# A loop of six turns for TensorE's value matmuls of the second token tile, and six diagonal buffers in place of four

## The reference

```python
ug = u_tab[ec]
vg = v_tab[ec]
act = jax.nn.gelu(jnp.einsum('thkd,td->thk', ug, xc).astype(jnp.float32), approximate=False)
w = (gc * act).astype(vg.dtype)
return jnp.einsum('thk,thkd->td', w, vg)
```

## Time and profile before

| what | value |
|---|---|
| time, median of 3 runs | 1499.05 us (1497.91 to 1499.57) |
| the profiled execution's own time | 1500.34 us |
| span of the profile of that execution | 1498.5 us |
| PE busy, share of the span | 1372.7 us, 92% |
| DVE busy | 788.3 us, 53% |
| gathers (DMA queue q0), share of 16 engines' span | 44.0% |

### The profile page before, as it was taken

One profiled execution on the slowest core, in us unless ns is written; L12 is line 12 of the kernel. 1 busy time (PEld: TensorE's weight loads), 2 busy tenths in 40 slices (PEclk: granted clock), 3 DMA queues, 4 the chain that ended last, 5 costly groups with the idle time before them and its releaser, 6 DMA issues.

```text
span 1498.5 us, 16481 instructions
## 1 busy us (share of the span) xinstructions
PE 1372.7 (92%) x6098; PEld 709.4 (47%) x6098; DVE 788.3 (53%) x1912; ACT 292.7 (20%) x714; POOL 349.1 (23%) x321
## 2 busy tenths in 40 slices
PE   6999999999999999999999999997997777778787
PEld 4887665443443443433566665543543233333332
DVE  2257665232332332323525788757676766767555
ACT  1435312000000000001324433221212121212112
POOL 0005303000000000000000346543544443444450
PEclk9999999999999999999999999999999998998999
DMA  9743789999999999999343699999999999999997
GB/s 382 301 160 128 282 331 354 400 427 426 426 423 425 424 426 427 426 426 426 141 168 113 247 421 420 420 421 421 421 421 420 422 421 422 421 421 422 421 421 290
DMA packets 65442, 551.32 MB, mean 368 GB/s; under 512 B 9265, under 2 KB 9537, under 8 KB 11857
## 3 DMA queue, kind: packets, MB, share of 16 engines
q1 hardware_dynamic: 26944, 278.06, 45.2%
q0 software_dynamic: 38416, 272.17, 44.0%
HBM read 549.16 MB, written 1.05 MB: 367 GB/s over the span
## 4 chain that ended last, share of the span: by engine, by line
PE 66%; DMA 28%; issue 2%; DVE 2%; ACT 1%; POOL 1%; SPq 0%; POOLq 0%; DVEq 0%; ACTq 0%
DMA ring<-peer_uv_d,work 18%; PE ps L2117 14%; PE ps L2015 12%; PE ps L2170 7%; PE ps L1354 6%; DMA work<-peer_uv_d,work 4%; PE ps L1843 4%; PE ps L1348 4%; PE ps L1804 4%; PE ps L2127 4%; DMA ring<-w_ada_d 2%; PE ps L1670 2%; DMA work<-expert_w_d 2%; DMA consts_sb<-peer_uv_d,work 1%; PE ps L1584 1%
## 5 line engine op out<-in xcount | busy, mean ns | idle before, releaser
L2015 PE MATMUL ps<-ring,work 128*128 128x512 f32 x604 | 288.1, 628 | 64.1 <-ACT work L1285 63.0
L3398 DVE CUSTOM_DVE_ANT_0 ring<-ring,work 128x1024 f32<-128x1024 f32 x152 | 186.7, 1229 | 121.4 <-DMA ring<-peer_uv_d,work 120.6
L2015 PEld LDWEIGHTS ps<-ring,work 128*128 128x128 f32 x604 | 116.8, 200 | 223.4 <-issue 136.3
L2350 POOL DMA_INDIRECT ring<-peer_uv_d,work x149 | 169.5, 1138 | 201.7 <-PE ps L2015 163.2
L2117 PE MATMUL ps<-ring,work 128*64 128x512 f32 x704 | 181.6, 592 | 0.5 <-DVE work L2914 0.5
L2015 PE MATMUL ps<-work 128*128 128x512 f32 x272 | 126.1, 610 | 21.6 <-ACT work L1285 21.6
L1285 ACT ACTIVATE work<-consts_sb,work 128x128 f32<-128x128 f32 x256 | 85.1, 392 | 280.2 <-DVE work L3407 278.9
L2117 PEld LDWEIGHTS ps<-ring,work 128*64 128x64 f32 x704 | 60.0, 137 | 99.7 <-issue 99.7
L3398 DVE CUSTOM_DVE_ANT_0 work<-work 128x1024 f32<-128x1024 f32 x68 | 83.3, 1225 | 45.3 <-DMA work<-peer_uv_d,work 44.7
L2322 POOL DMA_DIRECT2D mod<-subkeys_d x1 | 0.5, 546 | 454.9 <-DVEq L3006 454.9
L1354 PE MATMUL ps<-ring,hT 128*128 128x512 f32 (+1 forms) x256 | 105.7, 567 | 0.0
(11 more groups left out here) (500 smaller groups left out, 1809.8 us busy)
## 6 DMA issues: line engine op xcount, KB each, us to landing
ring<-expert_w_d SPq DMA_DIRECT2D x66, 2048.0 KB, 20.9
work<-expert_w_d SPq DMA_DIRECT2D x33, 1024.0 KB, 21.5
ring<-w_ada_d SPq DMA_DIRECT2D x12, 2048.0 KB, 9.9
ring<-w_in_d SPq DMA_DIRECT2D x11, 2048.0 KB, 20.5
consts_sb<-expert_w_d SPq DMA_DIRECT2D x11, 1024.0 KB, 20.0
ring<-w_out_d SPq DMA_DIRECT2D x4, 2048.0 KB, 8.1
mod<-expert_w_d SPq DMA_DIRECT2D x8, 1024.0 KB, 18.7
hT<-expert_w_d SPq DMA_DIRECT2D x8, 1024.0 KB, 21.1
```

Source lines behind the costliest of these rows:

```text
L2015: last = pe.matmul(ps[V_BANK[t] + n][:, :], diag[:, i % 4, :], v_row(i)[:, n * 512:(n + 1) * 512], start=(i % (16 * PH) == 0), stop=(i == ...
L2350: pool.indirect_dma_start(out=uv_rows(i), out_offset=None, in_=io["peer_uv"], in_offset=bass.IndirectOffsetOnAxis(ap=idx[:, s, k:k + 1], a ...
L3398: dve.tensor_tensor_reduce(out=u_row(i), in0=u_row(i), in1=h_tok[:, i // (16 * PH), :], scale=1.0, scalar=0.0, op0=ALU.mult, op1=ALU.add, ...
```

## The change

TensorE's picks 144 to 251 are no longer written out. `TURNED` is 256 - 3 - 1 - 108 = 144, and a loop of six turns (`TURNS`) goes over the 18 places. The 18 picks of the body wait for `diag_ready` at a value that is computed in a register from the turn. The argument `head_slot` asks that the loop's first instruction be loaded at the start of a block of instructions; a branch leads over the padding ahead of it. Picks 252 to 255 follow written out, as before. Since 18 is not a multiple of four, the body would need other buffers in each turn; there are now six diagonal buffers (`DIAGS`), and ScalarE waits for the pick six before. The `else` branch gets the same loop, and is not run.

```diff
+TURNS = 6
+TURNED = 16 * TT * PH - APART - 1 - UV_PLACES * TURNS
...
+DIAGS = 6
...
-        diag = W(6144, 4, P)
+        diags = [W(6144, 4, P)[:, i, :] for i in range(4)] + [W(12976, 2, P)[:, i, :] for i in range(DIAGS - 4)]
...
-                        if i + k - k0 > 3:
-                            act.wait_ge(v_free, i + k - k0 - 3)
-                        act.activation(diag[:, k % 4, :], ident, ACT.Copy,
+                        if i + k - k0 >= DIAGS:
+                            act.wait_ge(v_free, i + k - k0 - DIAGS + 1)
+                        act.activation(diags[(i + k - k0) % DIAGS], ident, ACT.Copy,
...
-                            last = pe.matmul(ps[V_BANK[t] + n][:, :], diag[:, i % 4, :], v_row(i)[:, n * 512:(n + 1) * 512],
+                            last = pe.matmul(ps[V_BANK[t] + n][:, :], diags[i % DIAGS], v_row(i)[:, n * 512:(n + 1) * 512],
...
-                values(at, 16 * N_STEP)
+                values(at, TURNED)
+                with nc.Fori(0, TURNS, engines=bass.OrderedEngineSet([pe.engine]), head_slot={pe.engine: 0}) as turn:
+                    for i in range(TURNED, TURNED + UV_PLACES):
+                        pe.wait_ge(diag_ready, turn * UV_PLACES + (i + 1))
+                        for n in range(2):
+                            last = pe.matmul(ps[V_BANK[1] + n][:, :], diags[i % DIAGS],
+                                             v_row(i)[:, n * 512:(n + 1) * 512], start=False, stop=False,
+                                             skip_group_check=True)
+                        last.then_inc(v_free, 1)
+                values(TURNED + UV_PLACES * TURNS, 16 * N_STEP)
```

More of the change, by code:

```diff
@@ L369 @@
 UV_PLAN = uv_plan(16 * TT * PH)
+TURNS = 6
+TURNED = 16 * TT * PH - APART - 1 - UV_PLACES * TURNS
+assert TURNED > 8 * TT * PH and all(UV_PLAN[i][0] == UV_PLAN[i + UV_PLACES][0]
+                                    for i in range(TURNED, TURNED + UV_PLACES * (TURNS - 1)))
+DIAGS = 6
+assert UV_PLACES % DIAGS == 0
 UV_TURN = [sum(UV_PLAN[m][0] == UV_PLAN[i][0] for m in range(i + 1)) for i in range(len(UV_PLAN))]
```

## The result

The changed kernel takes 1503.88 us (median of 22 runs, 1498.31 to 1505.65), the kernel before 1498.96 us (22 runs, 1497.91 to 1503.27). The ratio is 1.0023, with an interval of 1.0016 to 1.003: slower by about 3.4 us, where 1499.1 us was forecast. Of the 22 of the kernel before, one is above 1502. The profiled execution of the changed kernel took 1503.73 us, and its span is 1501.9 us, 3.4 us more than that of the profile before (whose execution, 1500.34 us, was itself 1.4 us above its median).

A forecast was written before the change was run, and what follows sets the result against it. DMA engines, full with gathers, were taken as the bound. Span 1498.5 us plus 0 (fetches, branches, registers) and 0.1 (end) made 1498.6; 1.84 around it, less 1.29 to the median, gave 1499.1 us, range 1497.2 to 1501.4.

The forecast's parts named there:

- the span of 1498.5 us: Whole program: the earlier profile's span, taken as the starting value to which the gather stage's terms were added.
- Fetches of code, gain 0: Gather stage: three TensorE code fetches fall on a DMA engine with time left; gain 0, at the other end 3.5 us.
- Rival C: Gather stage: the code fetches did cost, 1.15 us each, and three are gone; 1495.6 us, chance 0.05.
- Branches, 0 in the first five turns: TensorE's loop in the gather stage: 0.05 us a branch, at most 3.57 us, hidden by TensorE's rest; cost 0.
- The upper bound of 3.57 us: TensorE's loop branches: most one might take, from TensorE's own jump over the other branch at 1493.7 us.
- Register instructions: TensorE's loop: 18 register additions are 0.67 us a turn, at most 5.4 us, under the 9.5 us of rest; cost 0.
- The sixth turn, 0.1 us: End of the gather stage, where picks run without a pause: delays add up to 0 to 0.2 us, taken as 0.1.
- Rival B: End of the gather stage: a branch or register waits are dear, up to 2.1 us; 1500.5 to 1501.2 us, chance 0.08.
- The last jump: TensorE's jump at its end: still there, with 1.0 us to spare before SyncE's drain; no change.
- Six diagonals, 0: Gather stage: diagonals wait for VectorE's weights, so more buffers don't bring them earlier; 0.
- Rival A: Gather stage: as forecast, all hidden; 1499.1 us, 1497.9 to 1500.3 with scatter, chance 0.80.
- Rival D: Gather stage: TensorE's back edge waits for its code behind the gathers, up to 74 us slower, 1573 us; chance 0.03.

The follow-up runs named there:

- experiment 3: Changed kernel with the loop replaced by written-out picks in both branches, six diagonal buffers kept: 1498.9 us, ratio 1.0002 to the kernel before.
- experiment 1: Two added waits make GpSimd's first sums wait for VectorE: changed kernel 1499.11 us, ratio 0.9996; kernel before 1499.45 us, 1.0006.
- experiment 2: Kernel before with one added wait: VectorE starts two masks only when ScalarE has scaled the tile GpSimd then sums; 1505.19 us, ratio 1.0041.
- experiment 4: Changed kernel with the loop in one branch, the other written out: only where it runs 1503.9 us, ratio 1.0018; only where never run 1504.23 us, 1.0019.
- experiment 7: Never-run matmuls added: changed kernel (288) 1498.92 us, ratio 0.9993; loop only in the branch not run (160) 1499.2 us, 0.9994; kernel before (288) 1499.12 us, 0.9994.
- experiment 9: Changed kernel with both two waits added on GpSimd and 288 matmuls that never run: 1499.63 us, ratio 0.9996 to the kernel before.

## Why the prediction was wrong

The step that failed is its first sentence: "The change touches one stage, so I read the busy time by stretches first". All terms of the sum and all four rivals lay in the stage of the gathers, and the span of 1498.5 us went into the sum as it was: everything outside the stage was put at 0 without a reason. The runs showed in its place a loss in the head of the program, where the kernel before stood about 0.2 us (0.51 less the 0.30 us from mask to mask) from a meeting that costs 4.3 us. By TensorE's first matmul of the experts it had grown to 5.5 us, and 3.4 us were left at the end of the profile.

- *Fetches of code, gain 0:* right. The q8 packets fell from 51 to 49; from 1231 to 1492 us one is left, at the start of the loop, where the earlier trace rows has three. The dots stayed 2.48 us apart (1303.80 to 1306.28 after), and the step of the earlier trace rows stands as before, 3.39 us (1341.09 to 1344.48). Rival C is out: TensorE's code is fetched less and nothing was gained.
- *Branches, 0 in the first five turns:* right in the sum, too small in the size. The prediction took 0.05 us, and under 0.1 us as the sign of being right; a back edge took 0.21 to 0.23. The upper bound of 3.57 us did not hold the branch in, which took 5.41 us. Both are hidden. TensorE's run of 16 matmuls ahead of the loop began at 1221.35 and the loop's first at 1231.28, 9.93 us apart; the same two stand 9.92 us apart before (1217.90 and 1227.82). The run took 8.60 us, at a granted clock of 0.83, where it took 7.13 us at 1.00 before, and even so ScalarE's diagonal is what TensorE waits for in both.
- *Register instructions:* 32 ns each; no gap of the dots or of TensorE grew by them.
- *The sixth turn, 0.1 us:* 191.61 against 191.60 us from a dot to the last additions, so 0. The branch passed takes 76 ns, and TensorE rests 0.88 us before pick 253, as in the earlier trace rows (0.90). Rival B is out.
- *The last jump:* 3.64 us in place of 3.57, still hidden.
- *Six diagonals, 0:* right, by experiment 3.
- *Rival A* described its stage rightly and missed the time. *Rival D* gave the sign that was found, by luck, for a reason that was not: from issue to landing a gather takes 25.6 to 32.8 us, as in the earlier trace rows.

What stands in place of the failed step, and how far each link goes. That the loss is the meeting of two engines is shown from both sides: taken away with the loop in place (experiment 1), and made without it (experiment 2). That it comes with the length of TensorE's code, or with something that goes with it, whether run or not, is shown by experiments 4 and 7, with one gap: neither the filled kernels nor that with the waits ran beside the changed kernel as it is, and only their ratios to the kernel before link them. That the link between them is the landing of the weights fits all 15 profiles, since GpSimd came at most 0.25 us after the start of the first mask wherever they met, and at least 0.41 us after it wherever they did not; but each kernel has one profile, and no run moved the landing alone in a controlled way. How the length of code moves a landing by some tenths of a microsecond stays open. Open too is the rest of the scatter: executions above 1502 us are found of the kernel before as well, 17 of 136 over all comparisons, and no profile shows one of them. Some are left where GpSimd is made to wait, too (1 of 11 and 1 of 12, experiments 1 and 9), so this meeting isn't their only cause.

## What to carry to other kernels

A change that makes the program shorter can move the time in a part of the kernel that it doesn't touch: lay the two traces side by side from the start and look for the first row that differs, before looking at the code that was changed. Where GpSimd's sums run beside VectorE instructions with SBUF inputs, read the distance of their starts; if it is tenths of a microsecond, order them by a semaphore (here it cost nothing that the runs show, 1.0006), since otherwise each small edit may decide anew whether they meet. And when the runs of a kernel fall into two groups, compare how many fall into each, not the medians alone.

## What the runs showed of the hardware

- A pair of 128 x 256 products with two SBUF inputs takes 0.72 us, and 5.05 to 5.08 us if a GpSimd addition of 128 x 2048 (4.5 to 4.7 us) starts between them: 0.08 to 0.25 us after the first, in six profiles. At 0.41 us and more, in nine, there was no loss. An operation of VectorE with one large SBUF input and a column of scalars (TENSOR_SCALAR, 128 x 256, a pair of 0.61 us) was held too, to 5.25 us.
- In the first meeting GpSimd pays nearly nothing: 7.02 to 7.20 us for its two sums in the six profiles with a meeting, 6.97 to 7.15 in the nine without.
- On TensorE a taken branch back takes 0.21 to 0.25 us over 164 instructions, the first turns being the longer ones, and 0.22 to 0.25 over some 330. The passed one takes 76 ns, the branch into the loop 5.4 to 6.2 us, and a register addition 32 ns.
- 288 matmuls that are never executed made a kernel 5 us faster in the median (1503.88 to 1498.92 us, not measured beside each other; against the kernel before, measured beside each, 1.0023 and 0.9993).
